# Sample states of a hybrid decoder: stacked split-precision update, 32-column products, decay moved to ScalarE

## The reference

```python
xdt = chunk(x.astype(jnp.float32) * dt[..., None])
a_cs = jnp.cumsum(a, axis=2)
to_end = jnp.exp(a_cs[:, :, -1:] - a_cs)
states = jnp.einsum('bclgn,bclgrp->bcgrpn', bc.astype(jnp.float32), xdt * to_end[..., None])
chunk_decay = jnp.exp(a_cs[:, :, -1])
def step(h, inp):
    s_c, d_c = inp
    return h * d_c[..., None, None] + s_c, h
y_off = jnp.einsum('bclgn,bcgrpn->bclgrp', cc.astype(jnp.float32), h_prev) * jnp.exp(a_cs)[..., None]
y = y_diag + y_off
```

## Time and profile before

| | |
|---|---|
| median of 3 runs | 2349.39 us (2348.1 to 2352.71) |
| the profiled execution | 2350.6 us |
| its span, first to last instruction | 2348.9 us |
| mean clock granted to TensorE | 0.942 of full speed |
| busy: PE, PEld | 2146.5 us (91%), 1983.2 us (84%) |
| busy: DVE, ACT, POOL | 1282.1 us (55%), 985.2 us (42%), 64.0 us (3%) |

### The profile page before, as it was taken

One profiled execution on the slowest core, in us unless ns is written; L12 is line 12 of the kernel. 1 busy time (PEld: TensorE's weight loads), 2 busy tenths in 40 slices (PEclk: granted clock), 3 DMA queues, 4 the chain that ended last, 5 costly groups with the idle time before them and its releaser, 6 DMA issues.

```text
span 2348.9 us, 38021 instructions
## 1 busy us (share of the span) xinstructions
PE 2146.5 (91%) x14838; PEld 1983.2 (84%) x14838; DVE 1282.1 (55%) x2029; ACT 985.2 (42%) x1117; POOL 64.0 (3%) x86
## 2 busy tenths in 40 slices
PE   7999899888999988899989998989799998879996
PEld 5999898776788888899989998887688787869996
DVE  3453555665666574554355434566656665655533
ACT  3552434453333432554255434343533445235532
POOL 2000000000000000000000000000000000000000
PEclk9999999988999999999999999998889989989998
DMA  6544546413444334344434445543324442434441
GB/s 199 172 166 152 150 139 188 148 55 91 123 126 125 101 108 144 125 161 160 147 126 161 157 152 171 161 139 122 89 79 128 124 136 82 144 105 162 161 161 56
DMA packets 258376, 317.05 MB, mean 135 GB/s; under 512 B 9214, under 2 KB 232990, under 8 KB 258154
## 3 DMA queue, kind: packets, MB, share of 16 engines
q1 hardware_dynamic: 249800, 287.92, 38.2%
q0 software_dynamic: 7776, 26.73, 3.8%
q10 hardware_dynamic: 680, 0.80, 0.1%
HBM read 291.44 MB, written 26.33 MB: 135 GB/s over the span
## 4 chain that ended last, share of the span: by engine, by line
PE 81%; DVE 8%; ACT 5%; issue 2%; DVEq 2%; DMA 1%; SPq 0%; ACTq 0%
PE ps L1440 21%; PE ps L1442 20%; PE ps L1441 20%; PE ps L1541 4%; PE ps L1865 3%; PE ps L1861 3%; DVE w_lo L930 2%; ACT w_hi L683 2%; PE ps L1808 1%; PE ps L1525 1%; DVEq L1118 1%; PE ps L1518 1%; PE ps L1828 1%; DVEq L1322 1%; PE ps L1737 1%
## 5 line engine op out<-in xcount | busy, mean ns | idle before, releaser
L930 DVE TENSOR_TENSOR w_lo<-w_raw,w_hi 128x2048 fp32r<-128x2048 f32 x248 | 568.0, 2291 | 693.6 <-ACT w_hi L683 693.2
L1440 PE MATMUL ps<-u_hi,w_hi 128*128 128x288 f32 x2736 | 845.0, 309 | 39.4 <-DVE u_lo L957 31.6
L1441 PE MATMUL ps<-u_lo,w_hi 128*128 128x288 f32 x2736 | 829.8, 303 | 0.0
L1442 PE MATMUL ps<-u_hi,w_lo 128*128 128x288 f32 x2736 | 826.6, 302 | 0.0
L683 ACT ACTIVATE w_hi<-w_raw 128x2048 fp32r<-128x2048 f32 x249 | 476.8, 1915 | 652.7 <-PE ps L1442 629.8
L1440 PEld LDWEIGHTS ps<-u_hi,w_hi 128*128 128x128 f32 x2736 | 536.6, 196 | 48.5 <-issue 45.1
L1441 PEld LDWEIGHTS ps<-u_lo,w_hi 128*128 128x128 f32 x2736 | 537.3, 196 | 0.4
L1442 PEld LDWEIGHTS ps<-u_hi,w_lo 128*128 128x128 f32 x2736 | 537.0, 196 | 0.0
L1440 PE MATMUL ps<-h_hi,w_hi 128*128 (+1 forms) x704 | 208.5, 296 | 14.9 <-DVE w_lo L930 14.9
L1442 PE MATMUL ps<-h_hi,w_lo 128*128 (+1 forms) x704 | 207.4, 295 | 0.0
L1441 PE MATMUL ps<-h_lo,w_hi 128*128 (+1 forms) x704 | 207.3, 294 | 0.0
(11 more groups left out here) (266 smaller groups left out, 2442.2 us busy)
## 6 DMA issues: line engine op xcount, KB each, us to landing
w_raw<-in_ffn_w_dram SPq DMA_DIRECT2D x128, 1024.0 KB, 5.0
w_raw<-in_w_in_dram SPq DMA_DIRECT2D x82, 1024.0 KB, 5.3
h<-in_state_ssm_dram SPq DMA_DIRECT2D x32, 512.0 KB, 4.1
out_dram<-h POOLq DMA_DIRECT2D x32, 512.0 KB, 3.8
w_raw<-in_w_ssd_out_dram SPq DMA_DIRECT2D x16, 1024.0 KB, 4.9
kv_in<-in_cache_kv_w_dram SPq DMA_DIRECT2D x32, 256.0 KB, 4.4
w_raw<-in_w_o_dram SPq DMA_DIRECT2D x8, 1024.0 KB, 4.8
w_raw<-in_ffn_w_dram SPq DMA_DIRECT2D x8, 512.0 KB, 3.4
```

What stands on the lines that cost most here:

```text
L930: dve.tensor_tensor(w_lo[s][:], raw[s][:], w_hi[s][:].bitcast(F32), ALU.subtract)\
L1440: pe.matmul(out, wh, hi, start=first, stop=False)
L1441: pe.matmul(out, wh, lo, start=False, stop=False)
L1442: return pe.matmul(out, wl, hi, start=False, stop=last)
```

## The change

- **The update in fp32r.** The 32 rows of the product L1861 become 96: `x_split` holds the rounded `xdte_s` twice and the rest once, `b_split` rounded B, the rest of B, and rounded B again. `b_diag` is made from `b_split` with 96 partitions. One fp32r product over the 96 rows adds hi times hi, hi times lo and lo times hi. ScalarE writes one more copy of B, VectorE two copies and a difference for `x_split`, a difference and a copy for `b_split`, with drains between. `x_split` lies at R1, so VectorE waits for `conv_done_out` in the first group of a layer. The constant `c_small` is repeated three times.
- **The decay on ScalarE.** Behind each copy to `h0_t`, ScalarE multiplies the 8 old states in place by their decays (eight instructions of 128x128) and signals `h0_decayed`. VectorE waits for that too and adds the banks in one instruction of 1024 columns.
- **32 columns.** Each old state is multiplied with all 32 sample tokens instead of its own 4; `own_tokens` picks the own ones when VectorE reads the bank.

```diff
+SPLIT = 3
...
-    small = place("small", [TS, 2 * TS + NB])
+    small = place("small", [SPLIT * TS, 2 * TS + NB])
...
-    b_diag = r("b_diag", [TS, NB, NS])
+    b_split = r("b_split", [SPLIT * TS, NS], F32R)
+    b_diag = r("b_diag", [SPLIT * TS, NB, NS], F32R)
...
+    x_split = place("x_split", [SPLIT * TS, 256], F32R, at=R1)
...
-                    act.activation(b_tm_s[:], ps[0:TS, 7, 256:384], ACT.Copy).then_inc(b_ready.sem, 1)
+                    act.activation(b_tm_s[:], ps[0:TS, 7, 256:384], ACT.Copy)
+                    act.activation(b_split[0:TS], ps[0:TS, 7, 256:384], ACT.Copy).then_inc(b_ready.sem, 1)
...
                             .then_inc(h0_t_ready.sem, 1)
+                        for b in range(NB):
+                            state = h0[t % 3][:, b, :]
+                            last = act.activation(state, state, ACT.Copy, scale=e_s[:, t % 2, TS + b:TS + b + 1])
+                        last.then_inc(h0_decayed.sem, 1)
...
+                def own_tokens(t):
+                    products = ps[:, 3, 0:288] if t == 0 else ps[:, 1:3, :].rearrange("p k c -> p (k c)")[:, 256:544]
+                    return products.rearrange("p (b c) -> p b c", c=TS + NT)[:, :, 0:NT]
...
+                    dve.drain()
+                    if g == 0:
+                        wait(dve, conv_done_out, l, 32)
+                    dve.tensor_copy(x_split[0:TS], xdte_s[:])
+                    dve.tensor_copy(x_split[TS:2 * TS], xdte_s[:])
                     if g:
                         times_z(g - 1)
                     wait(dve, b_ready, l, g + 1)
-                    dve.tensor_tensor(b_diag[:], b_tm_s[:].unsqueeze(1).broadcast_to((TS, NB, NS)),
-                                      sel_s.unsqueeze(2).broadcast_to((TS, NB, NS)), ALU.mult)\
+                    b_hi = b_split[0:TS].bitcast(F32)
+                    dve.tensor_tensor(b_split[TS:2 * TS], b_tm_s[:], b_hi, ALU.subtract)
+                    dve.tensor_copy(b_split[2 * TS:], b_hi)
+                    dve.drain()
+                    dve.tensor_tensor(x_split[2 * TS:], xdte_s[:], x_split[0:TS].bitcast(F32), ALU.subtract)
+                    dve.tensor_tensor(b_diag[:], b_split[:].bitcast(F32).unsqueeze(1)
+                                      .broadcast_to((SPLIT * TS, NB, NS)),
+                                      sel_split.unsqueeze(2).broadcast_to((SPLIT * TS, NB, NS)), ALU.mult)\
                         .then_inc(b_diag_ready.sem, 1)
...
                         wait(dve, h0_product, l, tile + 1)
-                        for b in range(NB):
-                            dve.scalar_tensor_tensor(out=h0[tile % 3][:, b, :], in0=h0[tile % 3][:, b, :],
-                                                     scalar=e_s[:, t, TS + b:TS + b + 1],
-                                                     in1=ps[:, 6 + b // 4, (b % 4) * NS:(b % 4 + 1) * NS],
-                                                     op0=ALU.mult, op1=ALU.add)
+                        wait(dve, h0_decayed, l, tile + 1)
+                        dve.tensor_tensor(h0[tile % 3][:], h0[tile % 3][:],
+                                          ps[:, 6:8, :].rearrange("p k (b c) -> p (k b) c", c=NS), ALU.add)
                         dve.drain().then_inc(h_new_ready.sem, 1)
-                        dve.tensor_tensor(off_s[:, t, :], ps[:, 3 - 2 * t, 320:320 + TS], e_s[:, t, 0:TS],
-                                          ALU.mult)
+                        dve.tensor_tensor(off_s[:, t, :].rearrange("p (b q) -> p b q", q=NT), own_tokens(t),
+                                          e_s[:, t, 0:TS].rearrange("p (b q) -> p b q", q=NT), ALU.mult)
...
-                            pe.matmul(ps[:, 6 + n, :], xdte_s[:, t * P:(t + 1) * P],
+                            pe.matmul(ps[:, 6 + n, :], x_split[:, t * P:(t + 1) * P],
...
                         for b in range(NB):
-                            last = pe.matmul(ps[:, 3 - 2 * t, 320 + b * NT:320 + (b + 1) * NT], h0_t[:, b, :],
-                                             fc[:, TP + b * NT:TP + (b + 1) * NT], start=True, stop=True)
+                            last = pe.matmul(ps[:, 3 - 2 * t, 256 * t + b * TS:256 * t + (b + 1) * TS], h0_t[:, b, :],
+                                             fc[:, TP:T], start=True, stop=True)
                         last.then_inc(h0_product.sem, 1)
```

More of the change, by code:

```diff
@@ L173, in constants @@
     rows = (SCALE * (row_b[:, None] % 2 == np.arange(2)[None])).astype(f)
-    return {"c_square": sq, "c_small": small, "c_line": line, "c_line_mask": line_mask,
+    return {"c_square": sq, "c_small": np.tile(small, (SPLIT, 1)), "c_line": line, "c_line_mask": line_mask,
             "c_hot": hot, "c_mask": mask, "c_delta": delta, "c_rows": rows}
@@ L234, in trunk @@
     square = place("square", [P, 4, P])
-    small = place("small", [TS, 2 * TS + NB])
+    small = place("small", [SPLIT * TS, 2 * TS + NB])
     ident, ones, tri, sgt = (square[:, n, :] for n in range(4))
-    tri_sel_s, sel_s, tri_s, sgt_s = (small[:, 0:TS + NB], small[:, TS:TS + NB], small[:, 0:TS],
-                                      small[:, TS + NB:])
+    tri_sel_s, sel_split, tri_s, sgt_s = (small[0:TS, 0:TS + NB], small[:, TS:TS + NB], small[0:TS, 0:TS],
+                                          small[0:TS, TS + NB:])
     vec_a = place("vec_a", [P, P])
@@ L325, in trunk @@
     cbm = r("cbm", [P, 2, P])
+    b_tm_s = r("b_tm_s", [TS, NS])
     r = Plan(R1 + 16384)
@@ L336, in trunk @@
     xdte_s = r("xdte_s", [TS, 256])
-    b_tm_s = r("b_tm_s", [TS, NS])
-    b_diag = r("b_diag", [TS, NB, NS])
+    b_split = r("b_split", [SPLIT * TS, NS], F32R)
+    b_diag = r("b_diag", [SPLIT * TS, NB, NS], F32R)
     cbm_s = r("cbm_s", [TS, TS])
@@ L459, in trunk @@
         h0_t_ready = sem("h0_t_ready", KI)
+        h0_decayed = sem("h0_decayed", KI)
         h0_product = sem("h0_product", KI)
```

## The result

The changed kernel takes 2296.31 us (median, 2294.82 to 2297.33) against 2351.05 for the kernel before beside it: ratio 0.977 [0.975, 0.978], 55 us faster. The forecast was 2278, a gain of 71: the direction is right, the time lies in the range, and nearly a quarter of the gain is missing. The profiled execution took 2294.82, its span 2293.2, 55.7 less than the span before.

What follows compares the result with a forecast made beforehand. TensorE was taken to bound the state stage, partly at half clock. Step savings of 41.6 us plus 29.4 from the clock gave 71.0 off 2350.6, so 2279.6, median 2278; range 2264 to 2314.

Steps and rivals of the forecast that it cites:

- The update: L1861 on TensorE: two fp32r products take 0.48 us, not 1.91; saves 0.72 in visit 0, 1.43 in visit 1.
- Rival D: L1861: 96 rows in fp32r are no faster than 32 in fp32; 34.4 us lost, 2313; chance 0.06.
- The 32 columns: L1865 on TensorE: records stay 0.11 us apart with 32 columns, no cost; other end 29 us in all.
- Rival C: L1865: 32 columns cost L1813's spacing of 0.17 us; 29 of the 71 us are lost, 2307; chance 0.10.
- The decay: ScalarE behind h_t: eight in-place decays take 2.4 us per visit, nothing on the path; without that cover 0.5.
- the group's end: VectorE's addition becomes one instruction, 0.95 us shorter; L1808's wait of 0.9 goes in four groups, 3.6 us a layer.
- The split operands: VectorE between xdte_s and b_diag: 1.24 us, hidden with 0.1 to spare; otherwise 0.5 per group, 8 us in all.
- the wait for conv_done_out: VectorE, once a layer: the store lands by 552.3, VectorE arrives about 551.5, idle time follows; no cost.
- The clock: State stage: 9.5 of 12 half-clock units per layer come back, 1.55 us each, 14.7 a layer, 29.4 in all.
- Rival B: Behind visit 0: all nine half-clock units stay because hole and transposes stay; gain 50.9 us, 2298; chance 0.25.
- Rival E: State stage: half clock spreads to 6.8 us behind every visit, 109 us per layer; slower, 2370; chance 0.07.
- The signs that the prediction named: State stage: right if the mean clock is 0.96 or more; wrong if L1828 waits over 0.1 us for dec_s.

Runs made afterwards that it cites:

- run 4: Changed kernel with VectorE making b_diag behind dec and dec_s instead of ahead of them: 2296.55 us, ratio 0.977.
- run 8: Also called version 8: changed kernel with b_diag made behind dec and visit 1's side tile cut in two, half run before visit 0's update: 2261.48 us.
- Run 5: Kernel before the change, with only the products of the old states widened to 32 columns: 2346.42 us, ratio 0.998.
- run 6: Changed kernel reduced to the stacked update: 4 columns again and the decay on VectorE in eight instructions: 2302.73 us, ratio 0.979.
- run 11: Changed kernel with b_diag behind dec and the side tile cut in two, but the plain fp32 update on 32 rows: 2340.33 us, ratio 0.995.
- run 1: Changed kernel with the products of the old states back at 4 columns: 2307.94 us, ratio 0.982.
- run 3: Changed kernel with the decay back on VectorE in eight instructions of 128 columns: 2297.96 us, ratio 0.978.
- run 10: Changed kernel with b_diag behind dec and the side tile cut in two, but 4 columns: 2275.52 us, ratio 0.968.
- run 7: Changed kernel with 12 of the 24 products of visit 1's side tile moved between visit 0's turn and its update: 2269.58 us, ratio 0.965.
- run 2: Changed kernel with the update back in plain fp32 on 32 rows, without the split operands: 2342.17 us, ratio 0.996.

## Why the prediction was right and where it failed

**The update (L1861, now L1883): right.** Two products of 96 rows in fp32r take 0.47 us to the next start (forecast 0.48, bounds 0.46 to 0.85). Visit 1 saved 1.44 a group (1.43), visit 0 0.55 + 0.17 = 0.72 (0.72), with the wait for h_t that the sum had put there (0.64); the 0.17 is the update's start, 0.80 behind the start of the turn where it was 0.97. Together 17.3 us a layer, 17.2 forecast. Rival D is out.

**The 32 columns (L1865, now L1887): right in time.** 16 records from 616.30 to 618.10, 1.80 as before. Rival C is out.

**The decay: right.** Timeline of ScalarE, kernel after:

```profile
615.22 1.02 ACT L884 ACTIVATE h_t<-ps 128x1024 f32<-128x1024 f32 x1 [0.41 <-PE ps L1563]
616.14 2.43 ACT L888 ACTIVATE h<-h,e_s 128x128 f32<-128x128 f32 x8
```

2.43 us for eight, 2.4 taken. The Trainium skill ("ScalarE: Activation LUTs", What ACT_TABLE_LOAD costs) with its 93 ns per pointer operand had given an estimated 2.3; the trace agrees. VectorE waits for the decays in visit 0 only. The view puts its whole idle time, up to 2.2 us, down to them, but the old states' products end at 618.27 and the decays at 618.57, so 0.3 of it is theirs. Its addition takes 1.22 at 618.67, and the update of visit 1, which may overwrite the banks only after it, starts 3.5 later. At the group's end the wait of 0.9 is gone, 1.02 us in each of four groups: 4.1 a layer, 3.6 forecast.

**The split operands: this step failed.** The prediction took 1.24 us for them, put them beside 0.78 of idle time and 0.1 of spare, and left the other outcome, 0.5 a group and 8 us in all, in the bounds. That outcome came, with 0.6 a group and 9 us in all. Timeline of VectorE, first the kernel before, then after; the row of b_diag before stands in the earlier trace rows:

```profile
615.04 0.41 DVE L1255 TENSOR_TENSOR xdte_s<-xdt_s,to_end 32x256 f32<-32x256 f32 x1
615.38 0.74 DVE L1218 TENSOR_TENSOR flat<-flat,silu_z 128x576 f32<-128x576 f32 x1
```
```profile
605.76 0.40 DVE L1268 TENSOR_TENSOR xdte_s<-xdt_s,to_end 32x256 f32<-32x256 f32 x1
606.25 0.28 DVE L1275 CAST x_split<-xdte_s 32x256 fp32r<-32x256 f32 x1
606.55 0.28 DVE L1276 CAST x_split<-xdte_s 32x256 fp32r<-32x256 f32 x1
606.85 0.76 DVE L1227 TENSOR_TENSOR flat<-flat,silu_z 128x576 f32<-128x576 f32 x1
607.64 0.28 DVE L1281 TENSOR_TENSOR b_split<-b_tm_s,b_split 32x128 fp32r<-32x128 f32 x1
607.93 0.22 DVE L1282 CAST b_split<-b_split 32x128 fp32r<-32x128 f32 x1
608.22 0.42 DVE L1284 TENSOR_TENSOR x_split<-xdte_s,x_split 32x256 fp32r<-32x256 f32 x1
608.65 1.22 DVE L1285 TENSOR_TENSOR b_diag<-b_split,small 96x1024 fp32r<-96x1024 f32 x1
609.80 1.28 DVE L1292 TENSOR_TENSOR dec<-dec,cbm 128x512 f32<-128x512 f32 x2
611.00 0.27 DVE L1294 TENSOR_TENSOR dec_s<-dec_s,cbm_s 32x128 f32<-32x128 f32 x1
```

From xdte_s to b_diag it is 2.89 us after and 1.00 before: the split work costs 1.89. The forecast had let the copies overlap (0.20 of their 0.27). Here each takes its whole 0.30 from start to start, and silu_z's product, 0.66 from start to start before, takes 0.79 between them. dec has no idle time left in front of it, dec_s ends at 611.27, and L1850 waits 0.57. Runs 4 and 8 show the term by itself: moved behind dec, b_diag lets L1850 start 0.46 to 0.76 earlier. It was worth nothing at the clock of run 4 and 8.1 us in run 8. The other term beside it held: the wait for conv_done_out, put at nothing, is 0.2 us once in the layer (waits view, x_split L1275).

**The clock: direction right, size and reason not.** 9.5 of 12 units should come back, 7 did: visit 1's three as forecast, and four of visit 0's nine where 6.5 were judged. That is 2.5 x 1.55 = 3.9 us a layer. The reason given first was that the array streams eight times as many columns in L1865. Run 5 gives that part alone 5 us, and runs 6 and 11 put the larger part on the update: with 32 rows of plain fp32 the units are 10 to 12.6, whatever L1887 does. Visit 1's three units don't need the columns (run 1 has none behind visit 1). The columns add 5 us beside the stacked update (run 6 against run 3), 12 in the changed kernel (run 1, of which 6 have a place in the profile) and 14 where the hole is filled (run 10). The prediction named the shrinking update in the same sentence, with no size of its own; this was the step to weigh.

**Rival B** (2298) comes nearer to the measured time than the forecast, but not by its way: visit 0 kept five units, not nine, and the wait at L1850, which B doesn't have, makes up most of the rest. What B said of the place was right: all whole units that are left stand behind visit 0's hole, old states and turn, and run 7 took them away by dense products at that place. The Trainium skill ("TensorE: Matmul & The Clock Gate", Part 4) holds that transposes don't count as busy in the same way. No run here parts the turn from the hole beside it; version 8 still has 16 turns of states a layer and no drop behind any.

**Rival E** (slower) needed more half clock, and there is less than half of it.

The sum closes: -4.6 (dec_s) - 3.9 (units) + 0.5 (group ends) + 0.7 (0.09 in each step from visit 0 to visit 1, not foreseen; it goes again with the plain update of run 2) make the 7.3 us a layer between -35.5 and -28.2. With 28.6 saved in the second layer the two stages miss 14.1 of the forecast, and what lies outside them 1.2 more: the 15.3 by which the profiled execution's 55.7 falls short of 71. Outside the stage the spans differ by -1.7 ahead of the first one, +1.6 between the two and +1.4 behind the second. The first is a start at 546.53, where the twelve other profiles have 548.3 to 550.9, and isn't explained. Behind each stage there is more half clock than before: by the trace's clock records 93.3 us in place of 86.5 between the two stages and 44.0 in place of 40.7 behind the second. Windows view, 88.6 us behind the stage's end, kernel after and kernel before:

```profile
849.70:853.00 3.30, 3.30 (x16) 3.30 (x15) 0.88 (x1) 0.00 (x0) 0.00 (x0) 0.50 0.90 331
```
```profile
879.70:883.00 3.30, 3.30 (x25) 3.30 (x26) 2.29 (x1) 0.23 (x1) 0.00 (x0) 1.00 0.65 170
```

The same stretch of the feed-forward runs at 0.50 after and at 1.00 before, in code that the change doesn't touch. Why it falls there stays open.

**The signs that the prediction named.** Right: 0.47 behind L1883, the wait of about 0.7 for h_t, the spacing of 0.11, no wait of the segment product. Missed: a clock of 0.96 (0.95), and L1850 waiting 0.57 where over 0.1 was to mean trouble. That sign pointed at the step that failed. VectorE's waits for the decays, the sign of the group's end, came in visit 0 alone.

## What to carry to other kernels

Price small copies and casts in front of a shared wait at their whole distance from start to start, not at their overlapped one, and look for work to put ahead of them in the queue. Where a clock falls, read step lengths and half-clock stretches apart: an edit may save its step and lose it again to the clock, so try it once more when the clock is steady. Where half clock follows one place again and again, try dense products there that are in the program anyway: in run 7 twelve of them took away every whole unit, in run 11, beside the plain update, they didn't.

## What the runs showed of the hardware that was not expected

A group can last the same with more work or with less, because the clock makes up the difference. In run 3 the group takes 27.2 us (L1848 from 587.00 to 614.18), with the 0.90 wait and no half clock in groups 1 to 6; this is the windows view behind visit 0 of groups 1 and 2:

```profile
592.80:596.20 3.40, 3.40 (x31) 3.40 (x31) 2.74 (x11) 1.02 (x1) 0.00 (x0) 1.00 0.43 147
620.10:623.50 3.40, 3.40 (x31) 3.40 (x31) 2.23 (x9) 1.03 (x1) 0.00 (x0) 1.00 0.41 147
```

In run 4 the steps of a group sum to 25.8 us (with the 5.91 that the step between the visits takes at full clock in the table), and it takes 27.3 (half clock begins at 592.6, 619.9, 647.2) with 0.53 in the same stretches. TensorE did the same work ahead of both: update, hole of 0.64, old states, turn. What tells the two apart is not in the rows. (The expectation of run 6 gives 27.3 for run 3's group; from start to start it is 27.2.) That a hole of 0.9 us ahead of the segment product goes with a steadier clock behind visit 0 has been seen in runs 3 and 6 (2.7 to 4.7 units) and stays unexplained; whether the hole counts, or the length that it gives the group, no run parts.

The second surprise is the plain update: its 1.91 us in fp32 on 32 of 128 rows count as a busy TensorE in the windows view, and still half clock follows it. In its place 0.47 us in fp32r on 96 rows, alone (run 6), left 3.0 and 4.7 of 12.6 units. Whether it is the rows, the type or the length is not shown.
